# Second merge projection of a hybrid attention and state-space layer: two token halves of 256 columns per unit

## The reference

```
h = rms_norm(x, g_norm)
proj = h @ w_in                                   # (512, 2048) @ (2048, many)
q, k, v, att_gate, q_idx, k_idx, w_idx, u, ssm_gate, merge = split(proj)
att = dsa_attention(q, k, v, q_idx, k_idx, w_idx)
y_a = (att * silu(att_gate)) @ w_att_out
s   = gelu(s5_ssm(u, ...)); s = s * sigmoid(s @ w_glu + b_glu)
y_b = (s * silu(ssm_gate)) @ w_ssm_out
gates = sigmoid(merge + b_merge).reshape(b, l, 2, 2048)
mixed = gates[:, :, 0] * y_a + gates[:, :, 1] * y_b
out = rms_norm(x + mixed @ w_out, g_final)
```

## Time and profile before

| What | Value |
|---|---|
| Median of 3 runs | 1158.89 us |
| Profiled execution, its own time | 1159.37 us |
| Span of the profiled execution | 1157.6 us |
| TensorE, matmuls | 1129.8 us busy, 98% of the span, 5381 matmuls |
| TensorE, weight loads | 935.2 us busy, 81%, 5381 loads |
| VectorE | 727.3 us busy, 63% |
| ScalarE | 431.8 us busy, 37% |
| GpSimd | 38.6 us busy, 3% |
| Mean granted TensorE clock | 0.997 of full speed |

### The profile page before, as it was taken

One profiled execution on the slowest core, in us unless ns is written; L12 is line 12 of the kernel. 1 busy time (PEld: TensorE's weight loads), 2 busy tenths in 40 slices (PEclk: granted clock), 3 DMA queues, 4 the chain that ended last, 5 costly groups with the idle time before them and its releaser, 6 DMA issues.

```text
span 1157.6 us, 13437 instructions
## 1 busy us (share of the span) xinstructions
PE 1129.8 (98%) x5381; PEld 935.2 (81%) x5381; DVE 727.3 (63%) x1227; ACT 431.8 (37%) x565; POOL 38.6 (3%) x44
## 2 busy tenths in 40 slices
PE   5999999999999999999999999999999999999997
PEld 4899888888787788888777777888888888788885
DVE  4887558999736555626776888344234444777585
ACT  6522333332345452323223223332322221654374
POOL 4000000000000000000000000000000000000000
PEclk9999999999999999999999999999999999999998
DMA  8354454465642227456444765444657432577655
GB/s 253 83 137 109 118 162 121 111 145 110 170 121 57 90 73 175 109 141 160 140 133 122 161 144 126 148 130 161 146 128 162 110 90 66 189 249 270 234 190 203
DMA packets 188631, 166.35 MB, mean 144 GB/s; under 512 B 12868, under 2 KB 162712, under 8 KB 187928
## 3 DMA queue, kind: packets, MB, share of 16 engines
q1 hardware_dynamic: 167584, 129.97, 37.8%
q0 software_dynamic: 12800, 33.56, 13.1%
q10 hardware_dynamic: 8184, 1.95, 0.8%
HBM read 159.17 MB, written 37.75 MB: 170 GB/s over the span
## 4 chain that ended last, share of the span: by engine, by line
PE 84%; DVE 12%; ACT 1%; DMA 1%; issue 1%; SPq 0%; DVEq 0%; ACTq 0%
PE banks L518 21%; PE banks L520 21%; PE banks L519 21%; PE banks L763 4%; PE banks L765 4%; PE banks L764 4%; DVE w_lo L1199 2%; DVE score L1305 2%; DVE small L1304 2%; PE banks L670 2%; PE banks L651 1%; DVE score L1293 1%; DMA xt<-in_x 1%; PE banks L720 1%; PE banks L660 1%
## 5 line engine op out<-in xcount | busy, mean ns | idle before, releaser
L518 PE MATMUL banks<-act_hi,w_hi 128*128 128x512 f32 (+1 forms) x1088 | 421.6, 388 | 2.7 <-DVE w_lo L1199 2.7
L520 PE MATMUL banks<-act_hi,w_lo 128*128 128x512 f32 (+1 forms) x1088 | 416.8, 383 | 0.0
L519 PE MATMUL banks<-act_lo,w_hi 128*128 128x512 f32 (+1 forms) x1088 | 416.7, 383 | 0.0
L1199 DVE TENSOR_TENSOR w_lo<-w_raw,w_hi 128x2048 fp32r<-128x2048 f32 x80 | 183.2, 2290 | 95.6 <-ACT w_hi L865 94.7
L518 PEld LDWEIGHTS banks<-act_hi,w_hi 128*128 128x128 f32 x1088 | 204.4, 188 | 42.7 <-DVE w_lo L1199 4.3
L520 PEld LDWEIGHTS banks<-act_hi,w_lo 128*128 128x128 f32 x1088 | 204.2, 188 | 38.4
L519 PEld LDWEIGHTS banks<-act_lo,w_hi 128*128 128x128 f32 x1088 | 204.5, 188 | 34.8
L865 ACT ACTIVATE w_hi<-w_raw 128x2048 fp32r<-128x2048 f32 (+1 forms) x81 | 154.2, 1904 | 96.4 <-DMA w_raw<-in_w_in 96.3
L1615 DVE TENSOR_TENSOR w_lo<-w_raw,w_hi 128x512 fp32r<-128x512 f32 (+1 forms) x64 | 67.6, 1090 | 34.7 <-ACT w_hi L1105 34.7
L1105 ACT ACTIVATE w_hi<-w_raw 128x512 fp32r<-128x512 f32 (+1 forms) x64 | 59.8, 949 | 60.4 <-DMA w_raw<-w_sums 38.2
L1628 DVE TENSOR_TENSOR gate<-gate,yb 128x512 f32<-128x512 f32 x16 | 11.1, 692 | 83.5 <-ACT gate L871 83.5
(11 more groups left out here) (290 smaller groups left out, 1436.3 us busy)
## 6 DMA issues: line engine op xcount, KB each, us to landing
w_raw<-in_w_in SPq DMA_DIRECT2D x68, 1024.0 KB, 5.8
w_sums<-in_w_out POOLq DMA_DIRECT2D x24, 1024.0 KB, 8.3
w_raw<-w_sums SPq DMA_DIRECT2D x32, 512.0 KB, 4.1
w_sums<-w_sums POOLq DMA_DIRECT2D x8, 1024.0 KB, 11.4
w_raw<-in_w_att_out SPq DMA_DIRECT2D x8, 1024.0 KB, 5.3
w_raw<-in_w_out SPq DMA_DIRECT2D x16, 512.0 KB, 4.8
xt<-in_x SPq DMA_DIRECT2D x4, 1024.0 KB, 8.6
w_raw<-in_w_ssm_out SPq DMA_DIRECT2D x4, 1024.0 KB, 5.1
```

Source lines behind the costliest of these rows:

```text
L518: nc.tensor.matmul(out_ap, wh, x_hi[k], start=(j == 0), stop=False)
L519: nc.tensor.matmul(out_ap, wh, x_lo[k], start=False, stop=False)
L520: last = nc.tensor.matmul(out_ap, wl, x_hi[k], start=False, stop=(j == n - 1))
L1199: v.tensor_tensor(w_lo[:, u % SLOTS, :], w_raw[:, u % SLOTS, :], w_hi[:, u % SLOTS, :].bitcast(F32), ALU.subtract).then_inc(split_done, 1)
```

## The change

For the 14 units of `merge1` alone, TensorE no longer calls `body`. A new function does the same sums with the tokens cut into two halves of 256. It first goes through all 16 input tiles for the tokens 0 to 255, then through all 16 again for the tokens 256 to 511, into the two halves of the same bank. Each of the 48 weight blocks of a unit is thus loaded and used twice. The waits ahead of a unit and the one signal at its end stay. The two units of `merge1_first`, and everything on the other engines, stay as they are.

```diff
+            def merge1_by_halves(u, i):
+
+                slot, t = u % SLOTS, TILE0["merge1"] + i
+                wait_split(u)
+                pe.wait_ge(tile_free, t - 1)
+                for h in range(2):
+                    here = slice(h * HALVES, (h + 1) * HALVES)
+                    for k in range(KD):
+                        w = slice(k * P, (k + 1) * P)
+                        nc.tensor.matmul(stream_bank[t % 2][:, here], w_hi[:, slot, w], act_hi[:, k, here], start=(k == 0), stop=False)
+                        nc.tensor.matmul(stream_bank[t % 2][:, here], w_hi[:, slot, w], act_lo[:, k, here], start=False, stop=False)
+                        last = nc.tensor.matmul(stream_bank[t % 2][:, here], w_lo[:, slot, w], act_hi[:, k, here], start=False, stop=(k == KD - 1))
+                last.then_inc(tile_done, 1)
...
                 for i, u in enumerate(units(name)):
-                    unit(u, i)
+                    if name == "merge1":
+                        merge1_by_halves(u, i)
+                    else:
+                        unit(u, i)
```

## The result

The changed kernel takes 1167.85 us, the median of 3 runs (1167.28 to 1168.93), against 1158.89 us before. The ratio is 1.0078, with a 95% interval from 1.0056 to 1.0101: 0.8% slower. The forecast was 1167.9 us, with a range of 1163 to 1175.

A forecast was written before the change was run, and what follows sets the result against it. TensorE's stream of matmuls was taken to bound merge1. Cutting 672 matmuls in two at +0.0133 us each adds 9.0 us to the median of 1158.89, giving 1167.9 us, with a range of 1163 to 1175.

The forecast's parts named there:

- The bound: In merge1 the time is TensorE's stream of matmuls and nothing else; TensorE busy 152.65 of 153.00 us.
- The step of 256 columns: In merge1, 0.1200 us from one matmul's start to the next, against 0.2267 us at 512 columns.
- The straight line through 512 and 384: Steps of 0.2267 us in merge1 and 0.1733 in qidx, 0.0533 less per 128 columns, give 0.1200 for 256.
- its weakest joint: In merge1, a load every 0.120 us should hide, since 0.112 was kept up for sixteen; margin 0.008 us.
- The floor: At L699, sixteen matmuls of 128 columns, each with its own load, kept a step of 0.112 us.
- the hardest place for the loads: L699: sixteen matmuls of 128 columns, each with its own load, in 1.95 us.
- Rival one, no slower: In merge1 the surplus shrinks when matmuls and loads are short: 1161.1 or 1157.1 us; chance 0.09.
- Its 0.115 us for the pair: Two 256-column matmuls in a row in the k units take 0.23 us for two steps, 0.115 each.
- the rounds give the gained time back: In the k units, 512-column matmuls behind a pair return its gain: 2.98 us per round against 2.95.
- Rival two, a thin instruction stream: In merge1 TensorE needs an instruction every 0.060 us; if feeding falls short, 1181.3 us, very unlikely 1239.5; chance 0.09.
- Rival three, loads that bind: In merge1 each step takes the load's recorded 0.188 us: +100.4 us, 1259.3 us; chance 0.01.
- The waits: Around merge1 no wait is added, and the 0.84 us wait ahead of the output projection stays.

The follow-up runs named there:

- The quarters: The changed kernel with four pieces of 128 columns in place of two of 256 in merge1: 1307.35 us, ratio 1.1276 to the kernel before.

## Why the prediction was right

- **The bound.** It was read as TensorE's stream and nothing else in `merge1`. The table above shows it: the time follows the steps even at 148 us more, and both other engines only gained idle time.
- **The step of 256 columns.** The straight line through 512 and 384 gave 0.1200 us, and 0.1200 came out. The line was sound for this width and would have failed soon below: at 224 columns it gives 0.1067, where 0.1117 was measured, and at 128 it gives 0.0667 for 0.1117. The prediction called the loads its weakest joint, with a margin of 0.008 us, and that margin was real: by the law above, 256 lies 20 columns above the point where the line ends. That the same 0.0133 held one width further down owes something to luck: the prediction had no reason for it beyond two points, and with loads of 64 columns the surplus is not the same at 256 and at 512.
- **The reason behind the line** was only half right. The prediction said that the surplus belongs to "the matmul (or its load), not to the columns". With loads of 128 columns that holds from 512 down to 256. Halving the load showed a surplus of 0.0067 us at 256 columns, but of 0.0167 at 512. It depends on both, and the fixed 0.0133 holds for this load and not for every matmul. Why the cut costs is shown down to the step and no further.
- **The floor.** Its 0.112 us was read from sixteen matmuls and put at "one every 0.112 us has been kept up". The quarters kept 0.1117 through 2688 matmuls. Called "the hardest place for the loads", those sixteen are not: right behind them stand sixteen of the same shape with a step of (1.91 - 0.272) / 15 = 0.109 us, the last one's own duration taken off. And the eight of line 670 that stand together keep (1.06 - 0.277) / 7 = 0.112. Both rows are from the timeline of TensorE of the kernel before:

```profile
408.50 1.06 PE L670 MATMUL banks<-pT,v_tok 128*128 128x128 f32 x8
...
493.01 1.91 PE L704 MATMUL banks<-ident,b_blk 128*128 128x128 f32 x16
```

Line 704 transposes with the identity, and its loads are recorded with 141 ns in place of 191. So the 0.1117 is the floor for the matmuls of these projections, not for every matmul with a load of 128 columns. The Trainium skill, page "TensorE: Matmul & The Clock Gate", section "LDWEIGHTS (loading the stationary operand)", puts a load at its columns over 1.2 GHz. For 128 columns that is an estimate of 107 ns, for 64 columns of 53 ns. Read as the distance between loads, the runs agree within 5 ns at 128 columns and do not contradict it at 64 (a step of 0.0600); the recorded 192 ns of one load does not agree. The prediction took from it that 256 is the narrowest matmul that covers its load; with the surplus counted in, the measured law puts that at 236.

- **Rival one, no slower.** Its 0.115 us for the pair is the entry into narrow matmuls, not their pace. The changed kernel does the same on entering: its starts at 842.16, 842.28 and 842.39 are 0.23 us apart for two steps, and then the steps are 0.120. The reading that the rounds give the gained time back was right.
- **Rival two, a thin instruction stream,** is excluded by the 0.060 us steps. **Rival three, loads that bind,** was wrong in its price and, as far as the half loads show, right in kind: a load binds at 0.1117 us, not at the 0.188 us that it is recorded with. At 256 columns this floor did not bind yet, though the step there was not free of the load either (0.1133 us with half of it).
- **The waits.** The end of the stage moved by 8.95 us and the wait ahead of the output projection stayed at 0.84. A small miss: the loads are recorded with 192 ns on average, not the 188 that the prediction expected to stay.
- **The chances.** The forecast's own interval, 1163.4 to 1171.5 us, was given 0.80, and so was the wider range up to 1175, which also takes in part of the second rival. The wider one should have had a little more. Nothing else hangs on it.

## What to carry to other kernels

Where TensorE is the bound, price a cut of its matmuls by the distance between starts in a long uniform stretch, not by recorded durations: 0.2267, 0.1733 and 0.1200 us were the price here, while the durations of 389 and 282 ns would have priced a cut at 175 ns in place of 13. Before a line through two widths is drawn on to a third, ask where the other limit lies; in these projections a load of 128 columns allowed one matmul per 0.1117 us, and by the law worked out above everything narrower than 236 columns pays for columns that it does not stream. And a short run of a rare shape between others (two matmuls at 0.115 us) shows the way into a state, not the state. When a run changes the load, compare it with the uncut kernel that has the same load.

## What the runs showed of the hardware that was not expected

- The surplus over columns / 2.4 GHz is not one number. It is 0.0133 us at 256 to 512 columns with fp32r loads of 128 columns, 0.0067 us at 128 and 256 columns with loads of 64, yet 0.0167 us at 512 columns with the same loads of 64, and 0.0200 us with loads of 80. Reading only the upper 16 bits it is 0.0117 us at 512 columns and 0.0067 us at 256. No run here explains it; whether the stride of that last reading plays a part was not tried.
- A narrower load, with as many fewer channels written, can make a wide matmul slower: 512 columns with 64 output channels took 0.2300 us, with 128 channels 0.2267. With it the cut in two turns from a loss of 9.0 us into a gain of 2.4 (1160.8 to 1158.42).
- A load recorded with 192 ns can follow the one before it after 0.1117 us, and one recorded with 135 ns after 0.0600 us. The recorded time of a load says what it takes, not how often one can be had.
